# A decoder trunk on one core: the down projection's partial results reach the residual by ScalarE's copies and adding transfers instead of VectorE's adds

## The reference

```python
h2 = _rmsnorm(x, ffn_norm[l])
ff = jax.nn.silu(jnp.einsum('bsd,df->bsf', h2, w_gate[l])) * jnp.einsum('bsd,df->bsf', h2, w_up[l])
x = x + jnp.einsum('bsf,fd->bsd', ff, w_down[l])
```

## Time and profile before

| | |
|---|---|
| Median of 3 runs | 2178.67 us (2177.16 to 2179.44) |
| The profiled execution's own time | 2179.32 us |
| Its span in the profile | 2177.5 us |
| PE, PEld busy | 2160.8 us (99%), 1845.2 us (85%) |
| DVE, ACT, POOL busy | 1715.2 us (79%), 1083.4 us (50%), 22.2 us (1%) |
| DMA | 402.77 MB, mean 185 GB/s |

### The profile page before, as it was taken

One profiled execution on the slowest core, in us unless ns is written; L12 is line 12 of the kernel. 1 busy time (PEld: TensorE's weight loads), 2 busy tenths in 40 slices (PEclk: granted clock), 3 DMA queues, 4 the chain that ended last, 5 costly groups with the idle time before them and its releaser, 6 DMA issues.

```text
span 2177.5 us, 27179 instructions
## 1 busy us (share of the span) xinstructions
PE 2160.8 (99%) x10826; PEld 1845.2 (85%) x10826; DVE 1715.2 (79%) x1938; ACT 1083.4 (50%) x1144; POOL 22.2 (1%) x24
## 2 busy tenths in 40 slices
PE   9999999999999999999999999999999999999998
PEld 7899988888888888888888999888888888888886
DVE  5576774788898888889755867747888898888887
ACT  5454543554554544555453545435545554545544
POOL 0000000000000000000000000000000000000000
PEclk9999999999999999999999999999999999999999
DMA  7544455555665566566555434555665655565564
GB/s 251 179 135 130 141 177 184 181 197 194 200 200 196 193 202 202 193 202 201 191 176 174 139 115 154 176 188 181 199 200 194 204 199 193 194 206 197 195 206 159
DMA packets 221679, 402.77 MB, mean 185 GB/s; under 512 B 13440, under 2 KB 53664, under 8 KB 221472
## 3 DMA queue, kind: packets, MB, share of 16 engines
q1 hardware_dynamic: 220880, 400.90, 56.0%
q10 hardware_dynamic: 720, 0.78, 0.1%
HBM read 399.54 MB, written 2.10 MB: 184 GB/s over the span
## 4 chain that ended last, share of the span: by engine, by line
PE 95%; DMA 2%; DVE 1%; issue 1%; ACT 1%; SPq 0%; ACTq 0%; DVEq 0%; POOLq 0%; POOL 0%
PE bank L1015 19%; PE bank L1017 19%; PE bank L1016 19%; PE bank L694 10%; PE bank L696 10%; PE bank L695 10%; PE bank L654 2%; DMA stage<-in_w_in 1%; PE bank L819 1%; PE bank L760 0%; PE bank L883 0%; PE bank L871 0%; PE bank L761 0%; PE bank L762 0%; PE bank L770 0%
## 5 line engine op out<-in xcount | busy, mean ns | idle before, releaser
L1536 DVE TENSOR_TENSOR w_lo<-stage,w_hi 128x2048 fp32r<-128x2048 f32 (+4 forms) x319 | 679.6, 2132 | 269.0 <-ACT w_hi L1179 268.5
L1179 ACT ACTIVATE w_hi<-stage 128x2048 fp32r<-128x2048 f32 (+4 forms) x319 | 569.4, 1787 | 388.6 <-DMA stage<-in_w_down 192.2
L694 PE MATMUL bank<-w_hi,xt_hi 128*128 128x512 f32 (+4 forms) x1048 | 376.8, 359 | 6.1 <-DVE xt_lo L1597 4.3
L696 PE MATMUL bank<-w_hi,xt_lo 128*128 128x512 f32 (+4 forms) x1048 | 369.4, 352 | 0.0
L695 PE MATMUL bank<-w_lo,xt_hi 128*128 128x512 f32 (+4 forms) x1048 | 369.1, 352 | 0.0
L1015 PE MATMUL bank<-w_hi,xt_hi 128*128 128x512 f32 x812 | 316.5, 390 | 0.1
L1017 PE MATMUL bank<-w_hi,xt_lo 128*128 128x512 f32 x812 | 316.0, 389 | 0.0
L1016 PE MATMUL bank<-w_lo,xt_hi 128*128 128x512 f32 x812 | 315.9, 389 | 0.0
L1015 PE MATMUL bank<-w_hi,f_hi 128*128 128x512 f32 x696 | 271.3, 390 | 0.2 <-DVE f_lo L1945 0.2
L1017 PE MATMUL bank<-w_hi,f_lo 128*128 128x512 f32 x696 | 270.9, 389 | 0.0
L1016 PE MATMUL bank<-w_lo,f_hi 128*128 128x512 f32 x696 | 270.8, 389 | 0.0
(11 more groups left out here) (258 smaller groups left out, 2820.5 us busy)
## 6 DMA issues: line engine op xcount, KB each, us to landing
stage<-in_w_gate SPq DMA_DIRECT2D x176, 512.0 KB, 3.8
stage<-in_w_up SPq DMA_DIRECT2D x176, 512.0 KB, 4.7
stage<-in_w_down SPq DMA_DIRECT2D x174, 512.0 KB, 4.6
stage<-in_w_in SPq DMA_DIRECT2D x96, 384.0 KB, 3.7
stage<-in_w_out SPq DMA_DIRECT2D x64, 512.0 KB, 4.6
stage<-in_w_in SPq DMA_DIRECT2D x54, 512.0 KB, 4.5
stage<-in_w_in SPq DMA_DIRECT2D x16, 320.0 KB, 3.4
stage<-in_w_q_b SPq DMA_DIRECT2D x12, 384.0 KB, 3.7
```

The costliest lines, as they stand in the source:

```text
L694: pe.matmul(acc, a, wh[:, i, :], start=first and i == 0, stop=False)
L696: mm = pe.matmul(acc, b, wh[:, i, :], start=False, stop=last and i == len(kts) - 1)
L1179: act.activation(w_hi[s][:, 0:kts * cols], stage[s][:, 0:kts * cols], ACT.Copy).then_inc(hi_made[s], 1)
L1536: vec.tensor_tensor(w_lo[s][:, 0:kts * cols], stage[s][:, 0:kts * cols], w_hi[s][:, 0:kts * cols].bitcast(F32), ALU.subtract).then_inc(lo_ ...
```

## The change

For chunks 0 to 9 of each layer VectorE no longer adds the down projection's results. ScalarE copies each from its bank to one of four new SBUF buffers (`part_sum`; `copy_out`), and GpSimd issues a transfer that adds the buffer to `resid` (`add_part`, `accum_op=ALU.add`). TensorE's waits before it fills a bank again now count ScalarE's copies (`part_out`). ScalarE waits before it writes a buffer for the transfer that emptied it (`part_added`), and VectorE waits for all of them once a layer, before the last chunk's results are added. On ScalarE the copies of d2 and d3 and the two `f_hi` now stand ahead of the rounding of u2. `f_hi[1]` and `f_lo[1]` move in SBUF to make room.

```diff
-X_ADDS = ADDS * (1 + FF_CHUNKS)
+X_ADDS = 2 * ADDS
+COPIES = ADDS * (FF_CHUNKS - 1)
...
-        f_hi = [arena(f"f_hi{i}", [P, 4, SEQ], F32R, 4 * SEQ * (2 * i)) for i in range(2)]
-        f_lo = [arena(f"f_lo{i}", [P, 4, SEQ], F32R, 4 * SEQ * (2 * i + 1)) for i in range(2)]
+        f_hi = [arena(f"f_hi{i}", [P, 4, SEQ], F32R, 42 * SEQ * i) for i in range(2)]
+        f_lo = [arena(f"f_lo{i}", [P, 4, SEQ], F32R, 4 * SEQ + 42 * SEQ * i) for i in range(2)]
+        part_sum = [arena(f"part_sum{i}", [P, NCH], F32, 8 * SEQ + NCH * i) for i in range(4)]
...
                 def added(f, n):
 
-                    pe.wait_ge(x_added, layer * X_ADDS + 2 * ADDS + f * ADDS + n)
+                    pe.wait_ge(part_out, layer * COPIES + f * ADDS + n)
...
+                def copy_out(c, n0, chunk, turn=0):
+
+
+                    n = n0 + c
+                    act.wait_ge(used[n % 4], layer * QUADS + n // 4 + 2 + turn)
+                    for t in range(NT):
+                        i = c % 2 * 2 + t
+                        before = 16 * (2 * layer * (FF_CHUNKS - 1)) + chunk * 32 + c // 2 * 16
+                        if not (layer == 0 and n0 == U_SECOND + 8 and c < 2):
+                            act.wait_ge(part_added[i], before)
+                        act.activation(part_sum[i][:, :], bank[DOWN_BANKS[c][t]][:, :], ACT.Copy).then_inc(part_out, 1)
+
                 def down(f, n0, turn=0, sets=0, after_set=True):
+
                     for c in range(4):
                         if c == 0 and after_set:
                             silus(f + 1)
-                        prepare(n0 + c + LEAD, turn, sets,
-                                (lambda: ff_turn(f + 1, TURN_BANKS, 0)) if c == 3 else None)
+                        if c:
+                            copy_out(c - 1, n0, f, turn)
+                        if c == 3:
+                            copy_out(3, n0, f, turn)
+                            ff_turn(f + 1, TURN_BANKS, 0)
+                        prepare(n0 + c + LEAD, turn, sets)
...
                     if c == 2:
                         ff_turn(FF_CHUNKS - 1, TURN_BANKS, 1)
+                copy_out(3, U_PEEL + 8, FF_CHUNKS - 2)
...
+                def add_part(f, c):
+
+                    for t in range(NT):
+                        i = c % 2 * 2 + t
+                        pool.wait_ge(part_out, layer * COPIES + f * ADDS + NT * c + t + 1)
+                        pool.dma_start(resid[:, t, c * NCH:(c + 1) * NCH], part_sum[i][:, :], accum_op=ALU.add)\
+                            .then_inc(part_added[i], 16)
+
+                for f in range(FF_CHUNKS - 1):
+                    for c in range(4):
+                        add_part(f, c)
...
-                def add_down(c, n0, turn=0):
-                    n = n0 + c
-                    vec.wait_ge(used[n % 4], layer * QUADS + n // 4 + 2 + turn)
-                    for t in range(NT):
-                        part = resid[:, t, c * NCH:(c + 1) * NCH]
-                        vec.tensor_tensor(part, bank[DOWN_BANKS[c][t]][:, :], part, ALU.add).then_inc(x_added, 1)
-
                 def down(f, n0, turn=0, sets=0, after_set=True):
-
-                    def between():
-                        add_down(3, n0, turn)
-                        ff_turn(f + 1, TURN_BANKS, 0)
 
                     for c in range(4):
                         if c == 0 and after_set:
                             activate(f + 1, n0 - 8, turn)
-                        if c:
-                            add_down(c - 1, n0, turn)
-                        prepare(n0 + c + LEAD, turn, sets, between if c == 3 else None)
+                        prepare(n0 + c + LEAD, turn, sets,
+                                (lambda: ff_turn(f + 1, TURN_BANKS, 0)) if c == 3 else None)
...
-                add_down(3, U_PEEL + 8)
-                vec.wait_ge(x_added, layer * X_ADDS + X_ADDS)
+                for i in range(4):
+                    vec.wait_ge(part_added[i], 32 * (layer + 1) * (FF_CHUNKS - 1))
```

More of the change, by code:

```diff
@@ L417, in program @@
         down_made = sem("down_made")
+        part_out = sem("part_out")
+        part_added = [sem(f"part_added{i}") for i in range(4)]
         ms_made, rstd_made = sem("ms_made"), sem("rstd_made")
@@ L1135, in last_down @@
                         if not last and t == 1 and c >= 2:
-                            added(f, 4)
+                            need(x_added, X_ADDS, 2 * ADDS + 4)
                             norm_turn("norm1", range(2 * c - 4, 2 * c - 2), layer + 1)
@@ L1466, in _ @@
                         silus(FF_CHUNKS - 1)
+                    else:
+                        copy_out(c - 1, U_PEEL + 8, FF_CHUNKS - 2)
                     if c == 1 and layer == DEPTH - 1:
@@ L2128, in _ @@
                         activate(FF_CHUNKS - 1, U_PEEL, 0)
-                    else:
-                        add_down(c - 1, U_PEEL + 8)
                     if c == 1 and layer == DEPTH - 1:
```

## The result

The change made the kernel slower: 2231.78 us (2229.57 to 2234.16, 4 runs) against 2179.02 us (2177.16 to 2179.44, 4 runs), a ratio of 1.0244, 95% interval 1.0232 to 1.0256, or 53 us. I had forecast 2178.0 us and a range up to 2197.

The account below looks back on a forecast made before the run. TensorE's matmuls, end to end, were taken as the bound. With 0.7 us gained on `f_lo` and other parts costing 0, 2179.32 - 0.7 = 2178.6 against the profiled execution, 2178.0 us against the median; range 2175.5 to 2197.

Parts of the forecast that it names:

- What bounds the kernel: Whole loop: a 63.46 us turn is TensorE matmuls end to end, 0.227 us each; other engines can only lengthen it.
- The 0.7 us that I took as gained: TensorE's waits for `f_lo` in the feed-forward part: gain from relieving VectorE, with bounds 0 to 2.4 us.
- ScalarE's part: 160 copies from PSUM add 85 us, 4.2 us a turn; later u2 rounding cuts u4's margin from 1.17 to 0.57 us.
- GpSimd's and the DMA's part: 160 adding transfers: landing in 4.7 us against 5.9 allowed, u3's load 1.4 us later against 1.9 free; cost 0.
- The landing: Time from d1's copy end to its buffer being free for d3's: 4.7 us taken, bounds 2.6 to 7.6.
- rival A: Adds land late, ScalarE stops at d3's copies; decides from 5.9 us per transfer, 2178 to 2209 us. Chance 0.18.
- rival B: Adds delay the weights: u3 lands over 1.9 us later, 2178 to 2194 us. Chance 0.09.
- The rule on the shared port: GpSimd's transfer issue might be held off by a running VectorE instruction, up to 2.3 us; rows show no such delay.
- the other half of the rule: GpSimd can't write descriptors while VectorE holds the shared port in a two-port mode; would cost 20 us.
- Ends of layers: VectorE's adds of the last chunk start 2.2 us late, made good before the end; the kernel's end doesn't move.
- marks of a wrong forecast: ScalarE waits for `part_added`, u3's rounding starts over 7 us after the transposes, or a turn exceeds 63.7 us.

Follow-up runs that it names:

- experiment 2: Changed kernel without its adding transfers: GpSimd clears one cell in place of each, so chunks 0 to 9 never reach the residual. 2179.05 us, ratio 0.9995.
- 5: Kernel before the change, with only ScalarE's order altered: `f_hi` made ahead of u2's rounding; VectorE's adds stay. 2178.33 us, ratio 1.0002.
- experiment 8: Changed kernel with eight copy buffers; adds of d1 and d2 held until after u3 and u4 of the next turn, others at once. 2187.40 us, ratio 1.0042.
- Experiment 1: Changed kernel with eight copy buffers instead of four, so ScalarE never waits for an adding transfer of the same chunk. 2267.44 us, ratio 1.0405.
- experiment 6: Kernel before the change, VectorE still adding, plus 160 same-size adding transfers by GpSimd onto four spare tiles nobody reads. 2228.92 us, ratio 1.0246.
- experiment 10: Changed kernel with eight buffers; d0's adds at once, those of d1, d2, d3 after u3, u5, u7 of the next turn. 2187.93 us, ratio 1.0051.
- experiment 11: As experiment 10, but VectorE adds chunk 9's copies from their buffers, so 144 transfers instead of 160. 2181.01 us, ratio 1.0009.
- 3: Changed kernel with plain transfers of the same size that overwrite the residual instead of adding to it. 2192.23 us, ratio 1.0068.
- 4: Changed kernel with adding transfers of only 256 of each 512 columns; still 160 transfers. 2186.20 us, ratio 1.0031.

## Why the prediction was wrong

**What bounds the kernel.** Right. Without the transfers (experiment 2) the rest of the change is worth -0.05% (±0.1%); no relief of VectorE can be measured. The 0.7 us that I took as gained lies below what these runs can tell.

**ScalarE's part.** Right. The copies take 0.60 us each and 1.06 us in pairs, as taken (0.53 each, 1.06); ScalarE's busy time rose by 77.5 us (1160.9 - 1083.4) where I had 85. Its turn came as written until d3's copies. That u2's rounding moved costs nothing that can be measured (2 and 5).

**The step that failed: "GpSimd's and the DMA's part".** Three things in it.
1. *Which traffic meets which.* I set only d3's pair against u3's load. The pairs of d1 and d2 are still being carried by then, and with u2's load ahead of u3's the engines have 15.6 us of work in 15.3. u3 landed 9.7 us after the transposes in the turn shown and 8.5 to 10.8 in others, where 5.1 + 1.4 was taken and some 7 was free. The size was too small as well: 0.7 us of each engine for one add was taken, 1.4 as the high end, and 1.54 measured. But the size alone doesn't make the loss: in experiment 8 d3's pair, 3.1 us by that measure, meets u3's load by itself, u3 lands less than 1 us later, and the loop loses nothing. What failed is the number of transfers set against the load. That "the DMA share of 0.60 leaves room on the mean, but not during a load" was in the text, and the sum was never made over the window in which the three pairs come.
2. *The landing.* I took 4.7 us, that of a 512 KB load "under the same traffic". The adds took 6.5 us, and 3.3 to 9.2. Plain transfers took 5.1 and adds of half the columns 5.0, so both the add and the bytes count. Spacing the pairs doesn't shorten it (7.3 us in experiments 10 and 11), so the crowding among the adds isn't shown to be what makes it long.
3. *Two rivals as if apart.* At 6.5 us rival A gave 2189, and rival B gave at most 2194. Experiment 1 takes A away and the time rises; experiment 6 has no ScalarE wait for a buffer and loses the same 50 us. So B's traffic is the cause, and A a symptom of it, which even eased it. Their mechanisms were named rightly, their price too low: `f_lo` and u4 both stall, 1.04 and 1.36 us above the 0.23 us distance in the turn shown, and the 18 passages are longer by 1.5 to 4.3 us each.

**The rule on the shared port.** GpSimd's issues took 0.87 us each (the longest 1.25) and a pair 1.77 us, beside a VectorE that was busy for 73% of the span, so nothing held an issue up for an instruction of up to 2.3 us. By the Trainium skill, "SBUF — State Buffer", section "Who interferes with whom", `tensor_tensor` has no two-port mode and does not stall GpSimd's descriptors; this trace agrees. The 20 us that the other half of the rule would have cost are not in the loss: experiment 10 has the same 160 issues, and its loop loses nothing.

**Ends of layers.** Wrong by the same step, and hidden under the loop's loss: experiments 8 and 10 are 9 us above the kernel before with no stall in the loop, with a stall of 4.6 us and the lower clock behind it in experiment 8, and in experiment 11 7 of them are gone with the last chunk's transfers. In the changed kernel VectorE's first add of the last chunk is 15.9 us after the last transposes instead of 11.3, which is 4.6 us later where 2.2 was taken; from those transposes to the end it is 37.8 us instead of 36.6.

**What would show it.** All three marks of a wrong forecast came: ScalarE waits for `part_added`, u3's rounding starts 9.7 us after the transposes (mark: 7), and a turn takes 66.2 us (63.7).

**What stays open.** Why u3's load lands later beside full-width plain transfers than beside half-width adds, with less engine time (3 and 4): a bound on what the engines or the memory move in a stretch would be a rival to their time, and no run separates the two. And what part of an add's 1.54 us is its second fetch.

## What to carry to other kernels

Before transfers are added to a kernel that streams its weights, sum the engine time of *all* transfers over the busiest window between two landings that matter, in us of each engine, and hold it against the window's length; a mean share of 0.60 says nothing of it. Take it as a first test only: plain transfers made a load late at a share of 0.92. Count an adding transfer within SBUF at more than twice a plain one of the same bytes. And when a wait looks like the cause, ask what it holds back: here it slowed the very transfers that did the harm, and taking it away made things worse. The cure that keeps every byte was not more buffers but the moment of issue, one pair in two units.

## What the runs showed of the hardware

- An adding transfer of 256 KB within SBUF, issued by GpSimd, takes 144 packets (23040 / 160) and 1.54 us of each DMA engine; the plain one takes 80 packets and 0.67 us, and a load packet 88 ns against 0.111 x 16 x 2227.6 / 23040 = 172 ns of an add's.
- Beside them a 512 KB load took 9.1 us from issue to landing (891.61 to 900.70), where the same load took about 4.5 us before.
- After a stall TensorE may run at its lower level (1.2 GHz), or may not: in experiment 1 eight matmuls lie 0.43 us apart after the stall of 2.13 us before 930.24 (granted clock 0.52), and after one just as long before 726.25 the clock is 1.00. In experiment 8 it is 0.54 over the 5.5 us after 4.6 us. In the changed kernel the stalls of 1.0 to 1.4 us shown above left the clock at 1.00, but after two such close together (up to 2132.37 and 2134.25) come eight matmuls 0.41 to 0.43 us apart.
